# Two RMS norms whose sums, roots and reciprocals are taken with tokens on partitions, in a hybrid attention, long-convolution and expert block

## What is computed

```python
def rmsnorm(x, g):
    y = x * lax.rsqrt(jnp.mean(x * x, axis=-1, keepdims=True) + EPS)
    return y * g
for l in range(DEPTH):                      # DEPTH = 2
    hc = modulate(rmsnorm(xc, norm1_g[l]), ...)      # context tokens
    hl = modulate(rmsnorm(xl, norm1_g[l]), ...)      # latent tokens
    ...
    xl = xl + mod_l[2] * merge(...)                  # attention and Hyena branches, gated
    hl = modulate(rmsnorm(xl, norm2_g[l]), ...)
    xl = xl + mod_l[5] * channel_mixer(hl, l, ...)   # dense SwiGLU in layer 0, experts in layer 1
    ...
return rmsnorm(xl, final_g)
```

## Time and profile before

| what | value |
|---|---|
| median of 3 runs | 1778.02 us (1777.67 to 1779.5) |
| the profiled execution | 1778.41 us, of which span 1776.6 us |
| mean granted TensorE clock | 0.987 of full speed |
| busy share of the span: PE, PEld, DVE, ACT, POOL | 95%, 72%, 39%, 24%, 3% |
| layer 0's norm before the feed-forward | about 446 to 470 us |
| layer 1's first norm and Hyena inputs | about 831 to 890 us |

### The profile page before, as it was taken

The page is one execution under the profiler, slowest core; times in us unless marked ns, Lnnn a source line. Parts: engine busy times, 40 slices in busy tenths (PEclk is TensorE's granted clock), DMA queues, the critical chain, the costliest instruction groups (busy, mean ns, idle before and its releaser), DMA issues.

```text
span 1776.6 us, 38526 instructions
## 1 busy us (share of the span) xinstructions
PE 1690.8 (95%) x17640; PEld 1279.5 (72%) x17640; DVE 697.5 (39%) x989; ACT 420.3 (24%) x583; POOL 48.0 (3%) x60
## 2 busy tenths in 40 slices
PE   7999999999899999999999898999999998999986
PEld 3777766788688888886877788775666765776743
DVE  5447656444633333997764563211001010101012
ACT  4233244333422223223533543000000000000001
POOL 0000000002000000220000000000000000000000
PEclk9999999999999999999999998999999999999999
DMA  9731212125223333685322249989999999999995
GB/s 389 300 110 55 100 48 72 60 95 211 105 96 126 127 122 121 247 298 196 119 95 96 99 156 414 343 361 413 427 428 428 428 428 427 428 427 427 428 426 227
DMA packets 46753, 439.79 MB, mean 248 GB/s; under 512 B 5361, under 2 KB 5617, under 8 KB 12418
## 3 DMA queue, kind: packets, MB, share of 16 engines
q1 hardware_dynamic: 40034, 399.47, 56.2%
q0 software_dynamic: 5552, 34.90, 5.3%
q10 hardware_dynamic: 1008, 3.02, 0.4%
HBM read 433.83 MB, written 3.54 MB: 246 GB/s over the span
## 4 chain that ended last, share of the span: by engine, by line
PE 80%; DMA 8%; DVE 7%; ACT 2%; issue 2%; DVEq 0%; SPq 0%; ACTq 0%
PE psum L2250 19%; PE psum L1753 14%; PE psum L1755 13%; PE psum L1754 13%; PE psum L2269 9%; DMA expert_units<-in_moe_up 4%; DMA expert_units<-in_moe_w 2%; PE psum L2227 2%; DMA expert_units<-in_moe_up_rest 1%; ACT units_hi L711 1%; DVE units_lo L1087 1%; PE psum L1992 1%; PE psum L2014 1%; PE psum L1798 1%; DVE squares L1181 1%
## 5 line engine op out<-in xcount | busy, mean ns | idle before, releaser
L2250 PE MATMUL psum<-expert_units,gathered 128*32 128x256 f32 (+1 forms) x8064 | 408.3, 362 | 13.0 <-DMA expert_units<-in_moe_up_rest 6.2
L2250 PEld LDWEIGHTS psum<-expert_units,gathered 128*32 128x32 f32 x8064 | 289.2, 110 | 128.3 <-issue 12.4
L1753 PE MATMUL psum<-h_hi,units_hi 128*128 128x512 f32 (+1 forms) x928 | 344.9, 372 | 13.1 <-DVE h_lo L1169 6.2
L1755 PE MATMUL psum<-h_hi,units_lo 128*128 128x512 f32 (+1 forms) x928 | 336.2, 362 | 0.0
L1754 PE MATMUL psum<-h_lo,units_hi 128*128 128x512 f32 (+1 forms) x928 | 336.1, 362 | 0.0
L1087 DVE TENSOR_TENSOR units_lo<-raw_units,units_hi 128x2048 fp32r<-128x2048 f32 (+2 forms) x88 | 175.2, 1991 | 264.1 <-ACT units_hi L711 264.1
L711 ACT ACTIVATE units_hi<-raw_units 128x2048 fp32r<-128x2048 f32 (+2 forms) x88 | 147.2, 1673 | 415.6 <-PE psum L1755 360.9
L1753 PEld LDWEIGHTS psum<-h_hi,units_hi 128*128 128x128 f32 x928 | 176.6, 190 | 54.7 <-issue 23.0
L2269 PE MATMUL psum<-expert_units,expert_midT 128*32 128x256 f32 x3600 | 201.3, 380 | 12.2 <-DMA expert_units<-in_moe_w 10.0
L1755 PEld LDWEIGHTS psum<-h_hi,units_lo 128*128 128x128 f32 x928 | 176.4, 190 | 27.1
L1754 PEld LDWEIGHTS psum<-h_lo,units_hi 128*128 128x128 f32 x928 | 176.8, 190 | 24.2
(11 more groups left out here) (326 smaller groups left out, 1689.9 us busy)
## 6 DMA issues: line engine op xcount, KB each, us to landing
expert_units<-in_moe_up SPq DMA_DIRECT2D x64, 2048.0 KB, 30.3
expert_units<-in_moe_w SPq DMA_DIRECT2D x40, 2048.0 KB, 31.4
expert_units<-in_moe_up_rest SPq DMA_DIRECT2D x32, 1536.0 KB, 29.8
raw_units<-in_w_in SPq DMA_DIRECT2D x40, 1024.0 KB, 4.8
raw_units<-in_ffn_w SPq DMA_DIRECT2D x22, 1024.0 KB, 4.9
mod_units<-in_w_mod_rows POOLq DMA_DIRECT2D x20, 1024.0 KB, 6.0
raw_units<-in_ffn_w SPq DMA_DIRECT2D x16, 704.0 KB, 5.6
raw_units<-in_w_pab SPq DMA_DIRECT2D x16, 512.0 KB, 3.6
```

Source lines behind the costliest of these rows:

```text
L1753: MM(o, wh, xh, start=first, stop=False)
L1755: return MM(o, wl, xh, start=False, stop=last)
L2250: ins = MM(o[GRP * q:GRP * (q + 1), :], G[:, k, at, GRP * rr:GRP * (rr + 1)], W[:, kk, q, :], start=k == 0 and rr % 2 == 0, stop=k == DK - ...
```

## The change

For q = 1 and 2 the sum comes out with tokens on partitions: squares are the stationary operand and one column of ones the moving one, four products of one column for each of the three summands. Root and reciprocal then run on 128x4 numbers, and four products of 128 columns (the reciprocals, broadcast along the free axis, against the identity) spread them over all partitions into bank 7, from where DVE's first item step reads them. For norm 1 that spread stands inside `mod_units(5)`, behind the first of its four parts; for norm 2 between the 4th and 5th spectrum. Beside that: ACT squares block 2n as soon as DVE has added the first half of a unit; the last rounding of the output projection and of the down stage moves behind the squares; up unit 1 is interleaved with up unit 0, three blocks behind it, with its wait for `up_mid` at block 3; ACT takes root 2 ahead of the first spectra; DVE's low part of Hyena unit 1 moves from before the reciprocal's place in the down loop to behind it; only the 8 latent items stand ahead of the Hyena loop, and the 8 context items follow units 0 to 4 as 2, 2, 1, 2, 1; spectra use other banks.

```diff
+UP_LAG = 3
+CONTEXT_ITEMS = {0: (8, 10), 1: (10, 12), 2: (12, 13), 3: (13, 15), 4: (15, 16)}
+        inv = sb(top, "token_inverse", [P, TOK // P])
-            return (q + 2) % 8 if l else (0, 1, 2, 3, 6, 7)[q % 6]
+            return (2, 3, 4, 5, 6, 2, 0, 1)[q] if l else (0, 1, 2, 3, 6, 7)[q % 6]
             def norm_root(q):
+                if q:
+                    A(inv[:], PS[:, 7, 0:TOK // P], ACT.Sqrt, bias=eps[:, 0:1], scale=1.0 / D).then_inc(n_rt, 1)
+                    return
...
+                    norm_root(2)
                     for q in range(2):
                         spectrum_out(l, q)
-                    norm_root(2)
...
-                norm_hi(2 * l, SHIFT1, HH, 2 * (8 - early), DK if l else 2 * DK)
+                norm_hi(2 * l, SHIFT1, HH, 2 * (8 - early), DK - 2 * (8 - early) if l else 2 * DK)
...
-                    if l and n == 1:
-                        norm_hi(2, SHIFT1, HH, 2 * DK - 2, 2)
+                    if l and n in CONTEXT_ITEMS:
+                        norm_hi(2, SHIFT1, HH, CONTEXT_ITEMS[n][0], CONTEXT_ITEMS[n][1] - CONTEXT_ITEMS[n][0])
...
                 for n in range(WO_U):
-                    if l == 0 or n < 2:
+                    if n < WO_U - 1 and (l == 0 or n < 2):
                         hi(b["wo"] + n + 2, n % 2, b["wo"] // 2 + (n + 2) // 2)
                     if l == 0:
+                        act.wait_ge(wo_added, n + 1)
+                        norm_square(2 * l + 1, 2 * n)
                         act.wait_ge(evac, evb[l]["wo"] + n + 1)
-                        for k in range(2 * n, 2 * n + 2):
-                            norm_square(2 * l + 1, k)
+                        norm_square(2 * l + 1, 2 * n + 1)
+                        if n == WO_U - 1:
+                            hi(b["wo"] + n + 2, n % 2, b["wo"] // 2 + (n + 2) // 2)
...
             def norm_reciprocal(q):
+                if q:
+                    V_.reciprocal(inv[:], inv[:]).then_inc(n_inv, 1)
+                    return
+            def norm_row(q, s):
+                return PS[:, 7, s * L:(s + 1) * L] if q else rs[:, s * L:(s + 1) * L]
...
+                    if j == 0:
+                        dve.wait_ge(n_row, q)
                     STT(sq[:, it % 2, 0:L], X[:, k, s * L:(s + 1) * L], scale[:, k, s:s + 1],
-                        rs[:, s * L:(s + 1) * L], ALU.mult, ALU.mult).then_inc(n_t, 1)
+                        norm_row(q, s), ALU.mult, ALU.mult).then_inc(n_t, 1)
...
                     norm_reciprocal(2)
-                norm_lo(2 * l, SHIFT1, na1, HH, HL, end=2 * DK - 2 if l else None)
+                    lo(b["u"] + 1, 1)
+                norm_lo(2 * l, SHIFT1, na1, HH, HL, end=DK if l else None)
...
-                    if l and n == 1:
-                        norm_lo(2, SHIFT1, na1, HH, HL, 2 * DK - 2, 2 * DK)
+                    if l and n in CONTEXT_ITEMS:
+                        norm_lo(2, SHIFT1, na1, HH, HL, *CONTEXT_ITEMS[n])
...
-                    last.then_inc(evac, 1)
+                        last.then_inc(evac if j else wo_added, 1)
...
+            def token_sums(q, ks):
+                for k in ks:
...
+                    for c in range(TOK // P):
+                        last = MM(PS[:, 7, c:c + 1], squares[:, c * P:(c + 1) * P], ones[:, 0:1],
+                                  start=k == pooled[q] - 1 and c == 0, stop=k == DK - 1, skip_group_check=True)
+            def token_row(q):
+                pe.wait_ge(n_inv, q)
+                for c in range(TOK // P):
+                    last = MM(PS[:, 7, c * P:(c + 1) * P], inv[:, c:c + 1].to_broadcast([P, P]), ident, start=True, stop=True)
+                last.then_inc(n_row, 1)
...
+                    if i == LATE_TRIP and u == 0:
+                        token_row(1)
...
+                    if l and q == 4:
+                        token_row(2)
...
-                    streamed(1, 0).then_inc(unit_done, 1)
-                    up_second(0)
+                    for k in range(DK):
+                        pe.wait_ge(n_lo, items_before[1] + 2 * (k + 1))
+                        up_streamed(0, k)
+                        if k == UP_LAG:
+                            ready(b["up"] + 1)
+                            pe.wait_ge(up_mid, 1)
+                        if k >= UP_LAG:
+                            up_streamed(1, k - UP_LAG)
+                    for k in range(DK - UP_LAG, DK):
+                        up_streamed(1, k)
```

More of the change, by code:

```diff
@@ L367, in build @@
         out_done = sem("out_done")
+        n_inv, n_row = sem("n_inverse"), sem("n_row")
+        wo_added = sem("wo_added")
         o_ready, o_scaled, root_ready = sem("o_ready"), sem("o_scaled"), sem("root_ready")
@@ L955, in _ @@
                             u = b["down"] + 2 * m + n + 2
+                            if n and m == DK - 1:
+                                act.wait_ge(evac, evb[0]["down"] + m + 1)
+                                norm_square(2, m)
                             hi(u, n, u // 2, 11 * P if m < DK - 1 else 2048)
-                        act.wait_ge(evac, evb[0]["down"] + m + 1)
-                        norm_square(2, m)
+                        if m < DK - 1:
+                            act.wait_ge(evac, evb[0]["down"] + m + 1)
+                            norm_square(2, m)
                 else:
@@ L1465, in _ @@
                         last.then_inc(evac, 1)
-                        lo(b["down"] + 2 * m + 3, 1, 11 * P if m < DK - 1 else 2048)
+                        if m < DK - 1:
+                            lo(b["down"] + 2 * m + 3, 1, 11 * P)
                         mod_row_steps(8 * m + 3, 8 * m + 8)
@@ L1771, in features @@
                 return last
+            def token_sums(q, ks):
+                for k in ks:
+                    if k < pooled[q] - 1:
+                        continue
+                    if k == pooled[q] - 1:
+                        pe.wait_ge(n_add, adds_before[q] + pooled[q] - 1)
+                        squares = square_sum(q)
+                    else:
+                        pe.wait_ge(n_sq, 8 * q + k + 1)
+                        squares = sq[:, k % 2, :]
+                    for c in range(TOK // P):
+                        last = MM(PS[:, 7, c:c + 1], squares[:, c * P:(c + 1) * P], ones[:, 0:1],
+                                  start=k == pooled[q] - 1 and c == 0, stop=k == DK - 1, skip_group_check=True)
+                    last.then_inc(n_pe, pooled[q] if k == pooled[q] - 1 else 1)
+            def token_row(q):
[3 more added lines that the diff above has]
+                last.then_inc(n_row, 1)
             def norm_sums(q, ks=range(DK)):
+                if q:
+                    token_sums(q, ks)
+                    return
                 c0 = norm_c0[q]
@@ L1858, in filter_spectra @@
                         pe.wait_ge(evac, evb[0]["down"] + DK)
-                    reuse = 8 if l else 6
-                    if q >= reuse:
-                        pe.wait_ge(f_ac, 8 * l + 5 + q - reuse)
+                    if l and q == 5:
+                        pe.wait_ge(f_ac, 8 * l + 5)
+                    if l == 0 and q >= 6:
+                        pe.wait_ge(f_ac, 5 + q - 6)
                     o, g = q // 4, q % 4
@@ L2172, in up_second, with up_streamed @@
                         features(1, 2, 0, HH, HL).then_inc(unit_done, 1)
-                    up_second(0)
+                    def up_streamed(s, k):
+                        for j in range(2):
+                            last = mm3(PS[:, 2 * s + j, :], WH[:, s, cols(s, k, j)], WL[:, s, cols(s, k, j)],
+                                       HH[:, k, :], HL[:, k, :], k == 0, k == DK - 1)
+                        if k == DK - 1:
+                            last.then_inc(unit_done, 1)
+                    for k in range(DK):
[8 more added lines that the diff above has]
+                        up_streamed(1, k)
                     mod_turn(LATE_TRIP)
```

## The result

The changed kernel takes 1793.16 us (median of 4, 1791.24 to 1794.48) where the kernel before takes 1777.85 (median of 4, 1775.06 to 1779.5): ratio 1.0087, 95% interval 1.0069 to 1.0104, or 15.3 us slower. The profiled execution took 1794.48 us with a span of 1792.7, 16.1 over the span before. Slower was forecast, but by 8.1 us. Half of the loss has to be found.

The account below looks back on a forecast made before the run. PE, busy for 95% of the span, was taken to bound the kernel. Held PE 3.7 + clock 1.7 + layer 1 2.65 = 8.1 us on 1778.41 gave 1786.5, held to the median as 1786.1 us; range 1782 to 1790.

Parts of the forecast that it names:

- Norm 1 up to the items: Norm 1, sums to first item: reciprocals ready at 453.3 instead of 455.28, DVE's first item at 455.0 instead of 455.32.
- The held PE: Norm 1, interleaved up units: PE waits at block 3 for up_mid until 470.15, ends at 486.5 against 482.82, 3.7 us later.
- The clock behind the wait: Norm 1, after PE's wait at block 3: granted clock falls, costing 1.7 us more, bounds 0 and 3.4.
- the 486 to 488 named as a sign: Norm 1: PE through up unit 1 near 486 to 488 in the profile after.
- Norm 2: Layer 1, up to the Hyena units: PE starts unit 0 at 843.5 against 843.13, between 842.3 and 844.2.
- The Hyena loop: Layer 1: loop follows ACT and DVE, evictions 7.4 or 7.0 us apart against PE's 5.9; spectrum products 2.65 us later.
- the sign "less than 7 us": Hyena loop: the prediction is wrong if evictions come at less than 7 us.
- a bound of the prediction, not in its sum: Hyena loop: if the wait of 3 us at 883 brings the lower clock, up to 1.7 us more.
- the 2.65 of the sum: Layer 1's term: DVE's spectrum products start at 892.3 against 889.65, 2.65 us later; bounds 1.4 to 3.4.
- rival 2: Hyena loop: context items hide in DVE's and ACT's idle time, 3.8 us won; 1777.9 us, no change; chance 0.08.
- Rival 1: Norm 1: PE not held at block 3, through up unit 1 at 476.9, 5.9 us earlier; 1774.8 us; chance 0.05.
- Rival 3: Two more clock falls, at one-column products around 834 and the wait at 883, 1.7 us each; 1789.5 us; chance 0.12.

Follow-up runs that it names:

- e2: Kernel before plus an unused tensor of 4 floats, so everything behind it starts 32 bytes later: 1782.91 us, ratio 1.0051.
- e3: Kernel before plus an unused tensor of 16 floats, so everything behind it starts 64 bytes later: 1782.52 us, ratio 1.0041.
- e4: Kernel before with only the expert stage's tensors 32 bytes later: 1781.44 us, ratio 1.0047.
- e9: Kernel before with the expert stage's tensors 128 bytes later, some small ones moved to make room: 1779.8 us, ratio 1.0019.
- e11: e8 with the four new floats where the change has them, so all behind starts 32 bytes later: 1780.46 us, ratio 1.0028 to the kernel before.
- e8: e1 with both the early no-operation of e5 and the old context order of e7: 1774.66 us, ratio 0.9988 to the kernel before.
- e5: e1 with DVE's no-operation for up_mid put ahead of norm 1's 16 items: 1778.51 us, ratio 1.0013 to the kernel before.
- e1: Changed kernel with its four new floats in an existing tensor, every other tensor at its old address: 1787.03 us, ratio 1.0069 to the kernel before.
- e7: e1 with the old context order, 14 items ahead of the Hyena loop and 2 behind unit 1: 1779.93 us, ratio 1.0024 to the kernel before.
- e12: Kernel before with only the change's new order of context items: 1780.43 us, ratio 1.0036.
- e6: e1 with up unit 1 whole behind up unit 0, as in the kernel before: 1781.7 us, ratio 1.0032 to the kernel before.
- e10: Kernel before with the expert stage's tensors 512 bytes later, some small ones moved to make room: 1775.32 us, ratio 0.9998.

## Why the prediction was wrong

The direction and the two mechanisms held. What failed is the step that everything behind the two norms "is chained, so a delay is not made good later": the sum takes it to mean that what lies behind is only shifted and that the experts cost what they did before. They cost 4.7 us more, since a new tensor moved the addresses that their loads write.

- **The new tensor: not in the sum.** The prediction went through every instruction of the diff and never asked what the line that allocates `inv` moves. The expert stage costs 4.7 us more in the ledger. Over all profiles it takes 703.4 to 708.1 us (mean 705.9, nine kernels) with the slots at multiples of 256 bytes, 709.7 to 713.6 (mean 711.4, six) without: 5.5 us. From the first to the last expert product it is 634.8 to 637.3 us in the nine and 639.9 to 643.4 in the six. In time the shift alone costs 3.4 to 9 us (e2, e3, e4, e9, e11 against e8). This is the largest part of the 8 us that the sum missed; the rest, in the ledger, is 1.5 behind the products, 1.0 in norm 1, 0.4 in norm 2 and Hyena together, 0.3 between the two norms.
- **Norm 1 up to the items: forecast 455.0, measured 455.36.** The chain was as told (rounding, root at 451.47, low part, reciprocal in 0.17, spread). The spread was priced at 1.5 us from a row that I took as it stood and that had the lower clock for most of its length (0.51 from 896.4 to 899.0). It took 2.07 at the lower level here, and 1.05 at the full one in norm 2. A token sum, priced at 1.2, took 0.95 at the full level.
- **The held PE: forecast 3.7, right.** PE resumed at 470.03 (470.15 forecast); 16.3 us of products more would end at 486.3, 3.5 behind 482.82. e5 removes it.
- **The clock behind the wait: forecast 1.7 (0 to 3.4).** After: 489.27 - 486.3 = 2.9, close to the 3.0 that 6 us at a granted clock of 0.50 cost; PE is through later than the 486 to 488 named as a sign. In e1 and e7 norm 1 is 1.3 us shorter, so 1.6. Right as a term, and the profiled execution lay in the upper part of the bounds.
- **Norm 2: forecast +0.4, measured -0.54**, inside the bounds given (842.3 would be -0.8).
- **The Hyena loop.** Low parts start 7.28 and 6.88 us apart (forecast 7.4 and 7.0; the sign "less than 7 us" was drawn too close to that: 6.88 crosses it, though the mechanism is the one told), and PE's transposes 42.7 us behind unit 0 (forecast 42.8). But I let the products follow DVE's last eviction, and they wait for PE: 7.41 us behind the transposes, where it was 6.43, since the 2.96-us wait brought the lower clock (a bound of the prediction, not in its sum). Forecast 2.3 for unit 0 to products (48.8 against 46.52), measured 3.6. That norm 2 and the loop together came to 3.07, near the 2.65 of the sum, is luck: two errors of opposite sign.
- **The row that it was held against.** Of the ten profiles with the old context order seven have 45.0 us in the Hyena stretch, and three, the profiled execution before among them, 46.5. The lower clock comes either at unit 0 (840 to 848), where unit 2 has to wait for its eviction in any case and then waits 1.5 us for 2.97, or behind that wait (858 to 867), and only there it costs 1.5. So the 1.5 us of lower clock that rival 2 would have won are mostly not there to be won, and the new order's true price is 3.6 to 6.5. The stretch between the two norms shows the same: 348.3 to 348.6 us in three profiles (before, after, e12), which have the lower clock for 6.8 us in it (in the one before from 811.1 to 817.9), 346.6 to 347.1 in ten that have it for half as long, 345.5 in two that do not. So the one profile that the prediction was read from is some 3 us slower than most of its kind; its 1778.41 us stand against medians of 1775.05 to 1776.13 of the same kernel beside the experiments.
- **Rival 1, not held, 1774.8: its working was wrong.** Block steps left at 463.1 are 13, and PE can make five more by 470.1, which leaves 8 and not 5; PE has work without a pause (e5) and is through at 446.45 + 34.75 = 481.2, not 476.9. The interleaving is worth 1.6 us and not 5.9.
- **Rival 2, the items hide: no.** e12 shows them cost. **Rival 3, two more falls:** one came where it said (the wait ahead of the transposes), none at 834; one it did not name came at the sums of norm 1.

What stays open: the 1.5 us between the products and the expert loads. In twelve of the fifteen profiles this stretch is 179.7 to 179.8 us, in three 181.2 to 181.3 (after, e8, e12). Those three have the lower clock twice in it, shortly behind the products and at some place from 1035 to 1050; the others have it once. What decides that was not tried. Nor was it tried whether the sums in another form would keep the clock up.

## What to carry to other kernels

A new tensor is an edit to every tensor behind it: list the addresses before and after, and keep the slots that large loads land in at multiples of 256 bytes (5.5 us here). When an instruction is moved ahead of others in an engine's queue, move the credit that it waits for as well, or the wait takes along all that is queued behind. A gap on one engine is no room for more work if that work also occupies the engine that ends the gap: the context items filled DVE's idle time, and ACT, which does their middle step, then rounded the next unit later. And one profile is one draw of the clock: before a wait or a lower stretch is counted as a gain, see in a second profile whether it is there.

## What the runs showed of the hardware

**Load rate and address.** With slots at the old addresses or 256 or 512 bytes behind them 428 GB/s, at +32 and +64 bytes 424, at +128 bytes 425, with the DMA engines equally busy (1.01). The Trainium skill ("DMA: Bandwidth & Descriptors", section "How a descriptor splits into AXI transactions") says that a descriptor which does not start at a multiple of 256 bytes begins with a transaction from the boundary below, whose unused bytes still cost. That agrees with the step between 128 and 256 bytes. But the page tells it of bytes that are fetched, and here the side that moved is the one that the loads write; it gives no loss for large loads, and the runs show about 1%. That this is the mechanism is not shown by them.

**The clock.** The wait for the credit in norm 1 (5.03 us in after and e1, 4.21 in e7) came with the lower level in all three kernels that have it. So did the eight waits of 2.90 to 2.98 us in the Hyena stretch, for an eviction (before, e7, e8) or ahead of the transposes (after, e1, e5, e6, e12). The old norm 1's wait of 3.16 us, which I read as harmless because the profiled execution kept 1.00, comes with the lower level in four of eight profiles of it (e2, e4, e10, e12), and costs nothing in any: the stretch is 36.35 to 36.40 us in all eight. PE is fed by DVE there (0.18 us of waiting ahead of the fourth block), which I take for the reason. Between the one-column sums and the end of the spread the lower level came in all seven kernels that have them. The Trainium skill ("TensorE: Matmul & The Clock Gate", section "HAM oscillation — how this bites in real kernels") ties each such stretch, in the kernel that it describes, to a wait ahead of it. At the sums the row shows 0.84 us of waiting and no more, so by these runs a long wait is not needed for the fall.
